# The first microseconds of a two-layer block kernel: modulation and norm in four feature steps, the first weight unit walked in pairs of feature chunks

## What is computed

```python
def rms_norm(x, g):
    xf = x.astype(jnp.float32)
    y = xf * lax.rsqrt(jnp.mean(xf * xf, axis=-1, keepdims=True) + EPS)
    return (y * g.astype(jnp.float32)).astype(x.dtype)
def modulate(h, shift, scale):
    return h * (1.0 + scale) + shift
def swiglu(h, w_in, w_out):
    a, b = jnp.split(h @ w_in, 2, axis=-1)
    return (jax.nn.silu(a) * b) @ w_out
...
        mod_lat = (jax.nn.silu(c) @ w_mod[layer] + b_mod[layer])[:, None, :]
        mod_ctx = (jax.nn.silu(c_ctx) @ w_mod[layer] + b_mod[layer])[None, None, :]
        ml = jnp.split(mod_lat, N_MOD, axis=-1)
...
        x = x + 0.5 * ml[2] * swiglu(modulate(rms_norm(x, norm1_g[layer]), ml[0], ml[1]),
                                      ffn1_w_in[layer], ffn1_w_out[layer])
```

## Time and profile before

| | us |
|---|---|
| median of 3 runs (1348.61 to 1351.72) | 1351.22 |
| the profiled execution | 1352.08 |
| its span | 1350.3 |
| PE busy in the span | 1295.4 (96%) |
| DVE busy | 728.5 |
| ACT busy | 590.5 |
| GpSimd busy | 59.6 |

### The profile page before, as it was taken

The page is one execution under the profiler, slowest core; times in us unless marked ns, Lnnn a source line. Parts: engine busy times, 40 slices in busy tenths (PEclk is TensorE's granted clock), DMA queues, the critical chain, the costliest instruction groups (busy, mean ns, idle before and its releaser), DMA issues.

```text
span 1350.3 us, 23476 instructions
## 1 busy us (share of the span) xinstructions
PE 1295.4 (96%) x8912; PEld 1150.9 (85%) x8912; DVE 728.5 (54%) x1217; ACT 590.5 (44%) x885; POOL 59.6 (4%) x72
## 2 busy tenths in 40 slices
PE   5899999999999999999998999998999998999997
PEld 3677777778887799889998999997798888999997
DVE  2533333333333765776665555556467765756664
ACT  2443123422233446544445556545345564544542
POOL 1000000000001000000001000002013101000001
PEclk7899999999999999999998999997999999899998
DMA  9544444444224334423453554543532224455542
GB/s 390 214 186 154 172 175 187 170 174 185 87 71 157 116 134 160 152 94 116 165 189 121 222 199 172 189 161 117 187 125 94 94 98 151 156 187 187 186 161 88
DMA packets 30956, 214.13 MB, mean 159 GB/s; under 512 B 3376, under 2 KB 4656, under 8 KB 5936
## 3 DMA queue, kind: packets, MB, share of 16 engines
q1 hardware_dynamic: 30032, 209.73, 42.4%
q10 hardware_dynamic: 864, 3.56, 0.7%
HBM read 212.23 MB, written 1.05 MB: 158 GB/s over the span
## 4 chain that ended last, share of the span: by engine, by line
PE 86%; DVE 6%; ACT 4%; DMA 2%; issue 2%; DVEq 0%; ACTq 0%; SPq 0%
PE ps_u L1433 25%; PE ps_u L1434 25%; PE ps_u L1435 25%; PE ps_a L1408 2%; ACT w_hi L475 1%; PE ps_a L1391 1%; PE ps_a L1380 1%; DMA scr<-in_mods 1%; DMA raw<-in_stream 1%; DVE w_lo L815 1%; PE ps_a L1646 1%; DVE sq L871 1%; PE ps_a L1583 1%; PE ps_a L1568 1%; PE ps_a L1397 1%
## 5 line engine op out<-in xcount | busy, mean ns | idle before, releaser
L1433 PE MATMUL ps_u<-x_hi,w_hi 128*128 128x256 f32 (+1 forms) x1744 | 547.6, 314 | 19.5 <-DVE x_lo L882 10.5
L815 DVE TENSOR_TENSOR w_lo<-raw,w_hi 128x1024 fp32r<-128x1024 f32 x322 | 394.6, 1229 | 291.8 <-ACT w_hi L475 287.3
L1434 PE MATMUL ps_u<-x_lo,w_hi 128*128 128x256 f32 (+1 forms) x1744 | 539.6, 309 | 0.0
L1435 PE MATMUL ps_u<-x_hi,w_lo 128*128 128x256 f32 (+1 forms) x1744 | 538.9, 309 | 0.0
L475 ACT ACTIVATE w_hi<-raw 128x1024 fp32r<-128x1024 f32 x322 | 337.8, 1054 | 308.0 <-PE ps_u L1435 267.8
L1433 PEld LDWEIGHTS ps_u<-x_hi,w_hi 128*128 128x128 f32 x1744 | 337.8, 194 | 49.7 <-issue 28.8
L1435 PEld LDWEIGHTS ps_u<-x_hi,w_lo 128*128 128x128 f32 x1744 | 337.7, 194 | 15.7
L1434 PEld LDWEIGHTS ps_u<-x_lo,w_hi 128*128 128x128 f32 x1744 | 338.0, 194 | 15.1 <-issue 0.5
L1433 PE MATMUL ps_u<-h_hi,w_hi 128*128 128x256 f32 (+1 forms) x800 | 246.2, 308 | 0.5 <-DVE h_lo L956 0.5
L1434 PE MATMUL ps_u<-h_lo,w_hi 128*128 128x256 f32 (+1 forms) x800 | 245.2, 307 | 0.0
L1435 PE MATMUL ps_u<-h_hi,w_lo 128*128 128x256 f32 (+1 forms) x800 | 245.1, 306 | 0.0
(11 more groups left out here) (225 smaller groups left out, 806.4 us busy)
## 6 DMA issues: line engine op xcount, KB each, us to landing
raw<-in_stream SPq DMA_DIRECT2D x153, 1024.0 KB, 4.8
wide_scr<-in_mods SPq DMA_DIRECT2D x18, 1024.0 KB, 6.7
scr<-in_mods SPq DMA_DIRECT2D x18, 1024.0 KB, 6.8
raw<-in_stream SPq DMA_DIRECT2D x8, 768.0 KB, 4.1
x<-in_tokens ACTq DMA_DIRECT2D x2, 1024.0 KB, 14.6
wide_scr<-in_cmp_w SPq DMA_DIRECT2D x2, 1024.0 KB, 7.9
sq<-in_cmp_w SPq DMA_DIRECT2D x2, 1024.0 KB, 8.6
out<-x SPq DMA_DIRECT2D x4, 256.0 KB, 2.3
```

The costliest lines, as they stand in the source:

```text
L815: dve.tensor_tensor(w_lo[:, k % 2, cols], raw[:, k % 2, cols], w_hi[:, k % 2, cols].bitcast(F32), ALU.subtract).then_inc(l_ready, 1)
L1433: pe.matmul(dst, wh, xh, start=(kc == 0), stop=False)
L1434: pe.matmul(dst, wh, xl, start=False, stop=False)
L1435: ins = pe.matmul(dst, wl, xh, start=False, stop=(kc == span - 1))
```

## The change

The front goes in four steps of two feature chunks. The host lays the first eight blocks of `in_mods` out so that two blocks hold all contracted rows for scale and shift of two chunks; after blocks 0 and 1 the modulation of chunks 0 and 1 is complete. SP issues the tokens itself, ahead of everything, and unit 0 after the second block; a fifth landing slot is `raw[:, 1]`, the buffer of unit 1, so unit 1 is issued only when block 4 has been used. DVE instead of GpSimd adds up the squares, all eight chunks, so PE's sum over partitions is 4 matmuls instead of 12. Chunks 0 to 3 go as before but in pairs. For chunks 4 to 7 GpSimd forms `x*rstd` from a copy of the spread 1/rms in SBUF (`s1`), ACT applies scale and shift while rounding, and DVE computes `y` and subtracts. On PE unit 0 is walked in four steps; in each first both chunks of tile 0, then both of tile 1; modulation steps 2 and 3 stand between the quarters of the unit.

```diff
-MOD_FRONT = 2 * MOD_QUARTERS
+MOD_STEPS = 4
+MOD_FRONT = 2 * MOD_STEPS
...
-        mod_slots = (wide_scr[:, 0, :], wide_scr[:, 1, :], scr[:, 0:SLOT], scr[:, SLOT:2 * SLOT])
+        mod_slots = (wide_scr[:, 0, :], wide_scr[:, 1, :], scr[:, 0:SLOT], scr[:, SLOT:2 * SLOT], raw[:, 1, :])
...
-            for u in range(4):
-                mod_load(u, u)
-            load(0, 0, KD)
-            for u in range(4, MOD_FRONT):
-                sp.wait_ge(mod_done, u - 3)
-                mod_load(u, u - 4)
+            for i in range(2):
+                sp.dma_start(x[:, 4 * i:4 * i + 4, :], a["tokens"][:, 4 * i:4 * i + 4, :]).then_inc(x_landed[i], 16)
+            for u in range(MOD_FRONT):
+                if u > 4:
+                    sp.wait_ge(mod_done, u - 4)
+                mod_load(u, u % 5)
+                if u == 1:
+                    load(0, 0, KD)
+            sp.wait_ge(mod_done, 5)
             load(0, 1, KD)
-            def riding_load(p, n):
-                sp.wait_ge(mod_done, 4 * p + (MOD_FRONT + n - 3))
+            def riding_load(p, n, first=False):
+                sp.wait_ge(mod_done, MOD_FRONT + n - 2 if first else 4 * p + (MOD_FRONT + n - 3))
                 mod_load(4 * p + (MOD_FRONT + n), n % 4)
-            with sp.Fori(0, MOD_RIDE // 4 - 1) as p:
+            for j in range(4):
+                load(0, 2 + j, KD)
+                riding_load(0, j, True)
...
-            sums(0, NB)
+            pool.wait_ge(rb_copied, 1)
+            for kc in range(4, KD):
+                pool.tensor_tensor(sq[:, kc, :], x[:, kc, :], s1[:, 0, :], ALU.mult).then_inc(xr_ready, 1)
...
-            splits(0, 0)
-            act.wait_ge(mods_ready, 2)
-            norm_hi(0, NB, 0)
+            split(0, 0, 0)
+            norm_hi(0, NB, 0, kcs=(0, 1))
+            split(0, 0, 1)
+            norm_hi(0, NB, 0, kcs=(2, 3))
+            for kc in range(4, KD):
+                act.wait_ge(xr_ready, kc - 3)
+                act.wait_ge(scale_ready, kc // 2 + 1)
+                for seg, cols in segs(NB):
+                    ins = act.activation(x_hi[:, kc, cols], sq[:, kc, cols], ACT.Identity, bias=mods[:, kc, seg:seg + 1],
+                                         scale=am[:, 0, kc, seg:seg + 1])
+                ins.then_inc(xh_ready, 1)
...
+            def front_modulation(s):
+                dve.wait_ge(mod_done, 2 * s + 2)
+                half = MOD_COLS // 2
+                dve.transpose(turned[:, 0:half], ps_a[:, s % 2, 0:half]).then_inc(mod_turned, 1)
+                dve.wait_ge(mod_turned, s + 1)
+                both = turned[:, 0:half].rearrange("p (c t j) -> p c t j", c=2, t=2)[:, :, :, 0:2]
+                pair = slice(2 * s, 2 * s + 2)
+                bias = bm[:, 0:2 * KD].rearrange("p (c t) -> p c t", c=2)[:, :, pair].unsqueeze(3).broadcast_to([P, 2, 2, 2])
+                dve.tensor_tensor(mods[:, 0:2 * KD, :].rearrange("p (c t) j -> p c t j", c=2)[:, :, pair, :], both, bias, ALU.add)\
+                   .then_inc(mods_ready, 1)
+                dve.wait_ge(mods_ready, s + 1)
+                dve.scalar_tensor_tensor(am[:, 0, pair, :], mods[:, KD + 2 * s:KD + 2 * s + 2, :], 1.0,
+                                         vec[:, V_N1 + 2 * s:V_N1 + 2 * s + 2].unsqueeze(2).broadcast_to([P, 2, 2]), ALU.add, ALU.mult)\
+                   .then_inc(scale_ready, 1)
+                dve.wait_ge(scale_ready, s + 1)
...
+            def front_lo(kc):
+                dve.wait_ge(xr_ready, kc - 3)
+                y = t1[:, kc % 2, :]
+                for seg, cols in segs(NB):
+                    ins = dve.tensor_scalar(y[:, cols], sq[:, kc, cols], am[:, 0, kc, seg:seg + 1], mods[:, kc, seg:seg + 1],
+                                            ALU.mult, ALU.add)
+                ins.then_inc(y_steps, 1)
+                dve.wait_ge(y_steps, kc - 3)
+                dve.wait_ge(xh_ready, kc + 1)
+                dve.tensor_tensor(x_lo[:, kc, :], y, x_hi[:, kc, :].bitcast(F32), ALU.subtract).then_inc(xl_ready, 1)
...
+            for kc in range(1, KD):
+                dve.wait_ge(sq_ready, kc + 1)
+                if kc > 1:
+                    dve.wait_ge(sum_steps, kc - 1)
+                ins = dve.tensor_tensor(sq[:, 0, :], sq[:, 0, :], sq[:, kc, :], ALU.add)
+                ins.then_inc(sum_steps, 1) if kc < KD - 1 else ins.then_inc(sq_sums, SUMMED - 1)
             spread(0, 4)
-            modulation(0, 1, 0)
-            scale_of(0, 1, V_N1)
-            dve.wait_ge(scale_ready, 1)
-            splits(0, 0)
-            def after_scales():
-                modulation(1, 0, 1)
-            norm_lo(0, 0, NB, modulated(0, 1), 0, between=after_scales)
+            front_modulation(0)
+            split(0, 0, 0)
+            dve.wait_ge(rb_done, 1)
+            for s in range(2):
+                if s:
+                    front_modulation(s)
+                for kc in (2 * s, 2 * s + 1):
+                    norm_z(0, kc, NB, modulated(0, 1))
+                if s == 0:
+                    dve.tensor_copy(s1[:, 0, :], ps_a[:, 2, :]).then_inc(rb_copied, 1)
+                for kc in (2 * s, 2 * s + 1):
+                    norm_rest(0, kc, NB, 0)
+                if s == 0:
+                    split(0, 0, 1)
+            for s in range(2, MOD_STEPS):
+                front_modulation(s)
+                for kc in (2 * s, 2 * s + 1):
+                    front_lo(kc)
...
+            def front_step(s):
+                if s >= 2:
+                    pe.wait_ge(mod_turned, s - 1)
+                half = MOD_COLS // 2
+                for u in (2 * s, 2 * s + 1):
+                    pe.wait_ge(mod_landed[u % 5], LANDED * (u // 5 + 1))
+                    for i in range(4):
+                        for g in range(P // MOD_ROWS):
+                            rows = slice(g * MOD_ROWS, (g + 1) * MOD_ROWS)
+                            lo = (i * (P // MOD_ROWS) + g) * half
+                            ins = pe.matmul(ps_a[rows, s % 2, 0:half], sc_pad[:, 4 * (u % 2) + i, :], mod_slots[u % 5][:, lo:lo + half],
+                                            start=(u % 2 == 0 and i == 0), stop=(u % 2 == 1 and i == 3))
+                    ins.then_inc(mod_done, 1)
+            def front_unit():
+                pe.wait_ge(drained, 1)
+                for s in range(MOD_STEPS):
+                    if s >= 2:
+                        front_step(s)
+                    if s % 2 == 0:
+                        pe.wait_ge(l_ready, 5 + s // 2)
+                    for t in range(2):
+                        for kc in (2 * s, 2 * s + 1):
+                            pe.wait_ge(xl_ready, kc + 1)
+                            lo = kc * 2 * P + t * P
+                            wh, wl = w_hi[:, 0, lo:lo + P], w_lo[:, 0, lo:lo + P]
+                            pe.matmul(ps_u[:, t, :], wh, x_hi[:, kc, :], start=(kc == 0), stop=False)
+                            pe.matmul(ps_u[:, t, :], wh, x_lo[:, kc, :], start=False, stop=False)
+                            ins = pe.matmul(ps_u[:, t, :], wl, x_hi[:, kc, :], start=False, stop=(kc == KD - 1))
+                    if s % 2:
+                        ins.then_inc(halves_done, 1)
...
-                                unit(0, base + k + o, from_x(n), n, ready=normed(i))
+                                if k + o:
+                                    unit(0, base + k + o, from_x(n), n)
...
-            for u in range(MOD_FRONT):
-                mod(u, u // MOD_QUARTERS, u % MOD_QUARTERS, u % 4, LANDED * (u // 4 + 1), 0)
-                if u == 3:
-                    stat(0, 4)
-                if u == 5:
-                    spread(0, 4)
+            front_step(0)
+            pe.wait_ge(sq_sums, SUMMED - 1)
+            for t in range(4):
+                ins = pe.matmul(ps_a[:, 3, t:t + 1], sq[:, 0, t * P:(t + 1) * P], ones[:, 0:1], start=(t == 0), stop=(t == 3))
+            ins.then_inc(stat_done, 1)
+            spread(0, 4)
+            front_step(1)
+            front_unit()
```

More of the change, by code:

```diff
@@ L214, in program @@
         raw_landed = [sem("raw_landed0"), sem("raw_landed1")]
-        mod_landed = [sem(f"mod_landed{i}") for i in range(4)]
+        mod_landed = [sem(f"mod_landed{i}") for i in range(5)]
         cmp_landed = [sem("cmp_k_w_landed"), sem("cmp_v_w_landed")]
@@ L226, in program @@
         sq_ready = sem("squares_ready")
+        sum_steps = sem("front_sum_steps")
+        rb_copied = sem("front_rstd_copied")
+        xr_ready = sem("front_x_rstd_ready")
+        y_steps = sem("front_y_steps")
         sq_sums = sem("squares_summed")
@@ L465, in _ @@
             act.dma_start(cst[:, 0:K_R1], a["consts"][:, 0:K_R1]).then_inc(ident_landed, 16)
-            for i in range(2):
-                act.dma_start(x[:, 4 * i:4 * i + 4, :], a["tokens"][:, 4 * i:4 * i + 4, :]).then_inc(x_landed[i], 16)
             def split(pr, k, half):
@@ L505, in roots, with norm_hi @@
                    .then_inc(root_done, 1)
-            def norm_hi(i, n, shift, held=None):
```

(46 more changed lines are left out.)

32 lines of the change are left out of this document (19 added, 13 removed).

## The result

The changed kernel takes 1353.34 us in the median of 14 runs (1351.19 to 1356.27), the kernel before 1350.78 (14 runs beside it): ratio 1.002, 95% interval 1.001 to 1.0029. The forecast was 1353.6. A second set of 12 runs gave 1353.43 and 1.0026 (1.0012 to 1.004). The profiled execution took 1353.75, its span is 1351.7 (1350.3 before).

What follows compares the result with a forecast made beforehand. PE is busy from 53.8 us, so the end of unit 0 sets the time: -4.7 (timetable) + 4.6 (port turns) + 2.5 (clock) = +2.4 on 1352.1, 1354.5; the median 0.9 lower, 1353.6, range 1346.5 to 1358.5.

Steps and rivals of the forecast that it cites:

- Block cost: Modulation blocks on PE, now 32 records of half the columns: 2.0 us at the slow clock, 1.3 at the fast.
- Up to 1/rms: Front from block 1 done at 15.9 through sum, root, reciprocal and diagonals: spread of 1/rms done at 21.2 us.
- Steps 0 and 1 as if alone: DVE's z, copy, x_lo, weight half and second modulation without GpSimd's interference: done at 30.3 us, PE at 32.3.
- GpSimd's four products: In the front, they take turns with DVE's x_lo and weight half on the shared port: 4 x 1.15 = +4.6 us.
- The rings: Steps 2 and 3 run PE, DVE and ACT in series, 8.4 us each, with PE idle for 2.4 and 0.5.
- Clock: PE's gaps in unit 0 make the clock fall once, slowing nine matmuls and half of two blocks: +2.5 us.
- rival 4: In unit 0 the clock falls in every ring, with port turns: +7.7 us, 1358.9; chance 0.15.
- Moved queues: Unit 1's later load and those behind it land by about 43, used at 46 and 49: cost 0.
- 1: In the front DVE keeps the port, and the clock falls once: -2.2 us, 1349.0; chance 0.17.
- 2: In the front DVE keeps the port, and the clock doesn't fall: -4.7 us, 1346.5; chance 0.14.
- 3: In the front DVE and GpSimd take port turns, no clock fall: -0.1 us, 1351.1; chance 0.13.
- 5: Unit 1 is held by something else, so gain or loss up to 53.8 is taken up: 1351.2; chance 0.07.

Runs made afterwards that it cites:

- run with late products: Changed kernel, but GpSimd's four products wait until DVE has issued x_lo of chunks 0 to 3; ratio 1.0002 to the kernel before.
- doubled: Changed kernel, but GpSimd makes each of its four products twice, the extra result not used; 1356.66 us, ratio 1.0042 to the kernel before.
- undone: Changed kernel without GpSimd's part: DVE forms z of all eight chunks, no copy of 1/rms; 1351.05 us, ratio 1.0001 to the kernel before.
- the order alone: Changed kernel with PE's modulation blocks of steps 2 and 3 one step ahead; 1341.08 us, ratio 0.9938 to the kernel before.
- run with filler: Changed kernel with extra matmuls, results not used, in PE's gaps in unit 0; 1352.52 us, ratio 1.0013 to the kernel before.
- the delay: Kernel before with seven additions on DVE, results not used, ahead of its first x_lo; 1355.27 us, ratio 1.0035 to the kernel before.

## Why the prediction was right, step by step

| step | forecast | measured |
|---|---|---|
| Landings: block 1 there | 14.0 | 13.8 |
| Squares added | 12.9 | 13.25, hidden |
| Block cost, slow and fast | 2.0, 1.3 | 1.94, 1.05 |
| spread of 1/rms done | 21.2 | 21.1 |
| `x_lo` of chunk 3 done | 35 | 34.46 |
| gaps in steps 2 and 3 | 2.4 + 0.5 each | 3.33 + 0.36, 2.82 + 0.40 |
| port turns | +4.6 | +4.1 |
| clock in unit 0 | +2.5, one fall | +4.4, three on the path |
| first riding block | 56.2 | 58.45 |
| what is behind it | unchanged | -1.6 at the second norm |

*Landings, Squares, Block cost, Up to 1/rms* held (the squares' own terms, 7.8 and 4.9, give 12.7 and not 12.9; it changes nothing, the step is hidden). Twice the weight loads cost nothing; a fast block was even cheaper than I took, which gave 0.5 us a ring back. *Steps 0 and 1 as if alone* held: in the run with late products `x_lo` of chunk 3 ends at 30.4, forecast 30.3.

*GpSimd's four products* was the step with the least support, two places far away, and the mechanism is confirmed from three sides: moved (-4.16), doubled (+2.93, of which 2.1 are turns), undone. The price was 0.5 lower, as a product beside DVE held it for about 1.05 (3.04 us over three `x_lo`, 1.07 in the weight half).

*The rings* were right in kind: the gaps stand where forecast, and go with the order alone. Two of their terms were off and nearly cancelled: from the scale to the first `x_lo`, by way of ACT, it took 1.7 us (41.05 to 42.75) and not 0.9, and the pair of blocks 2.0 and not 2.6. In the run with filler, at the fast clock, the rings take 8.8 and 8.4 us; the forecast was 8.4. Without turns and clock the block would be at 58.45 - 4.1 - 4.4 = 49.95, forecast 49.1.

*Clock* is the mis-sized term. I took one fall for 2.5 from a single gap of 2.0 us; with gaps of 1.7 to 3.3 us in every step the clock fell in every step, for some seven matmuls each time and not nine. That was the mechanism of rival 4, whose clock terms summed to 7.8 us; it cost 4.4. What hid the miss was outside the sum: 1.6 us saved behind the second norm's sum of squares. So at the front I was 2.2 us low (+4.6 for +2.4; ring +0.9, clock +1.9, turns -0.5), and the median came within 0.3 us of the forecast by luck, because two misses cancelled. The mechanism of turns and ring is mine; that the clock fell in every step is rival 4's. *Moved queues* cost nothing: unit 1 starts at 59.66, right behind the riding block.

Of the rivals, 1 and 2 (DVE keeps the port) fall by the late products, 3 (no fall) by the windows, 5 (the front doesn't matter) by the delay and by the later runs, whose times roughly follow the riding block (41.25 and 1337.7, 45.41 and 1341.1, 54.29 and 1350.8, 61.38 and 1356.7).
